# A two-layer convolution and expert-retrieval encoder on one core: the first stage reordered, the adaLN rows in column tiles, the pooling on TensorE

## The reference, cut to what matters

```python
mod = silu(c) @ w_ada[l] + b_ada[l]                  # 1024 -> 6*1024: sh1, sc1, g1, sh2, sc2, g2
h = rmsnorm(x, norm_mix_g[l]) * (1 + sc1) + sh1
# layer 0
p = h @ w_in                                         # 1024 -> 512 + 512 + 512
a = a_lin * sigmoid(a_gate)
a_conv = depthwise_causal_conv(concat(prev_a, a), dw_a) + db_a        # 31 taps
a_out = silu(layernorm(a_conv, ln_g, ln_b))
pooled = multiscale_pool(concat(prev_b, b_in)) - b_in                 # means over 2, 4, 8, 16 tokens, by group
b_out = einsum('btgc,gcd->btgd', pooled, w_pool) * pool_scale         # (near the start the mean is over fewer)
y = concat(a_out, b_out) @ w_out
x = x + g1 * y
h = rmsnorm(x, norm_ffn_g[l]) * (1 + sc2) + sh2
x = x + g2 * peer(h, wq, k1, k2, u, v)               # queries, top-16 keys, gelu(u.h), weighted sum of v
```

## Time and profile before

| what | before |
|---|---|
| median of 3 runs | 4036.21 us (4035.36 to 4036.81) |
| the profiled execution | 4037.75 us |
| its span | 4036.0 us |
| mean granted TensorE clock | 0.973 |
| PE busy | 3816.7 us (95%) |
| PEld busy | 2994.3 us (74%) |
| DVE busy | 2563.5 us (64%) |
| ACT busy | 1024.1 us (25%) |
| POOL busy | 120.8 us (3%) |

### The profile page before, as it was taken

How to read it: one execution, slowest core, us unless ns; L and a number is a source line. 1 busy time by engine, 2 the same in 40 slices (tenths; PEclk the granted TensorE clock), 3 DMA queues, 4 the chain that set the end, 5 groups by cost and what they waited for, 6 DMA issues and landing times.

```text
span 4036.0 us, 72731 instructions
## 1 busy us (share of the span) xinstructions
PE 3816.7 (95%) x31704; PEld 2994.3 (74%) x31704; DVE 2563.5 (64%) x3885; ACT 1024.1 (25%) x950; POOL 120.8 (3%) x61
## 2 busy tenths in 40 slices
PE   8819889999999999999997989999999999999998
PEld 2302468888888888888883548888888888888886
DVE  1370277556665588888874438556566758888886
ACT  1300133332333311111113123333333321111111
POOL 0190000000000000000000000000000000000000
PEclk9859989999999999999998989999999999999999
DMA  7305222454654764545431311436456484545450
GB/s 277 126 23 196 87 84 90 177 187 154 212 188 157 273 240 190 212 184 198 181 134 63 116 64 64 147 137 206 165 204 198 168 322 183 200 182 215 183 192 33
DMA packets 196223, 667.08 MB, mean 165 GB/s; under 512 B 11952, under 2 KB 151360, under 8 KB 152512
## 3 DMA queue, kind: packets, MB, share of 16 engines
q1 hardware_dynamic: 190608, 663.67, 44.6%
q10 hardware_dynamic: 5392, 0.56, 0.1%
q0 software_dynamic: 32, 0.01, 0.0%
HBM read 514.72 MB, written 149.49 MB: 165 GB/s over the span
## 4 chain that ended last, share of the span: by engine, by line
PE 91%; DVE 3%; POOL 3%; DMA 2%; ACT 1%; issue 0%; SPq 0%; DVEq 0%; ACTq 0%; POOLq 0%
PE PS L691 35%; PE PS L647 33%; PE PS L568 5%; PE PS L622 5%; PE PS L591 4%; PE PS L551 3%; PE PS L677 3%; POOL arena L1016 2%; DVE ring L1096 1%; PE PS L578 1%; DMA arena<-gates_dram 1%; PE PS L635 1%; PE PS L597 1%; DMA arena<-act_dram 1%; DVE stat L1071 0%; ACT H L782 0%
## 5 line engine op out<-in xcount | busy, mean ns | idle before, releaser
L647 PE MATMUL PS<-X,ring 128*128 128x272 f16 x12288 | 1436.9, 279 | 0.0
L691 PE MATMUL PS<-arena,ring 128*128 128x272 f16 x12288 | 1423.7, 279 | 2.9 <-DVE ring L1096 2.9
L691 PEld LDWEIGHTS PS<-arena,ring 128*128 128x128 f16 x12288 | 1202.2, 98 | 224.4 <-issue 3.5
L647 PEld LDWEIGHTS PS<-X,ring 128*128 128x128 f16 x12288 | 1198.8, 98 | 218.7 <-issue 0.4
L1096 DVE SCALAR_TENSOR_TENSOR ring<-ring 128x4096 f16<-128x4096 f32 x145 | 641.3, 4424 | 634.8 <-ACT ring L791 626.3
L791 ACT ACTIVATE ring<-ring 128x4096 f16<-128x4096 f32 x145 | 523.9, 3615 | 1119.6 <-PE PS L691 1119.6
L1365 DVE TENSOR_TENSOR ACC<-PS,ACC 128x544 f32<-128x544 f32 x512 | 362.9, 719 | 237.1 <-PE PS L691 237.1
L921 ACT ACTIVATE H<-PS 128x544 f32<-128x544 f32 x256 | 159.9, 625 | 974.3 <-PE PS L647 974.3
L1355 DVE TENSOR_TENSOR arena<-arena 128x544 f32<-128x544 f32 x256 | 292.1, 1141 | 46.0 <-DMA arena<-act_dram 46.0
L622 PE MATMUL PS<-X,ring 128*128 128x272 f16 x1536 | 188.1, 284 | 38.2 <-DVE X L1103 38.2
L622 PEld LDWEIGHTS PS<-X,ring 128*128 128x128 f16 x1536 | 150.2, 99 | 73.2 <-issue 43.9
(11 more groups left out here) (136 smaller groups left out, 1821.8 us busy)
## 6 DMA issues: line engine op xcount, KB each, us to landing
ring<-U SPq DMA_DIRECT2D x64, 2048.0 KB, 10.5
ring<-V SPq DMA_DIRECT2D x64, 2048.0 KB, 7.9
act_dram<-H SPq DMA_DIRECT2D x64, 1088.0 KB, 5.0
gates_dram<-ACC SPq DMA_DIRECT2D x68, 1024.0 KB, 5.7
arena<-gates_dram SPq DMA_DIRECT2D x32, 2176.0 KB, 9.5
arena<-act_dram SPq DMA_DIRECT2D x64, 1088.0 KB, 5.1
ring<-whole_w SPq DMA_DIRECT2D x28, 2048.0 KB, 7.8
ring<-split_w SPq DMA_DIRECT2D x17, 2048.0 KB, 7.8
```

What stands on the lines that cost most here:

```text
L647: mm = pe.matmul(ps_halves(u)[:, half, :], parts[lane][:, pu, k * 512 + j * P:k * 512 + (j + 1) * P], H16[:, ph, k, half * HALF:(half + 1) ...
L691: mm = pe.matmul(ps_halves(u)[:, half, :], parts[lane][:, pv, j * D + c * P:j * D + (c + 1) * P], WT[:, grp, pw, j, half * HALF:(half + 1) ...
```

## The change

The first stage gets another order, and three of its parts another form.

- TensorE runs four adaLN slots (`EARLY`: `sh1` and `sc1` of layer 0), then five chunks of the input projection (`LEAD`), then seven more with one slot ahead of each (`BETWEEN`), then the other thirteen slots. `mod` of both layers is finished by `rest_of_mod` on VectorE behind the LayerNorm.
- The rows of a slot go to four column tiles: the conditioning vectors are padded with zeros to 32 columns, and k goes to the PSUM partitions 32 (k mod 4) and on. The turning product adds the four tiles up, with a 128 x 2 pick matrix in place of the identity.
- The convolution runs in two halves of two channel chunks, the first as soon as chunks 0, 1, 4 and 5 are read.
- GpSimd no longer pools. TensorE adds up shifted products of EB with `w_pool`/window (and `w_pool`/window - `w_pool` for the unshifted one); the first 16 tokens, where the mean is over fewer, go through a small pooled copy that VectorE makes (`corners`).
- The output projection does the half over the pooling channels (k 4 to 7) of its first four chunks ahead of and between the LayerNorm's sums; `Z` from VectorE completes them.
- adaLN slots past the fourth land in four places of their own (`ada_at`: two in the arena, H, and ring slot 1). The keys' tile holds the small tables until the keys are loaded, which waits for the last turn. The two split lanes change places.

```diff
+EARLY = 4
+LEAD = (0, 1, 2, 4, 5)
+BETWEEN = (3, 6, 7, 8, 9, 10, 11)
+POOL_AFTER = {13: 0, 14: 1, 15: 2, 17: 3}
...
# SyncE
+            def load_ada(s):
+
+                i = s % 4
+                if s >= EARLY + 4:
+                    sp.wait_ge(mm_done, ROW_AT[s - 4] + 1)
+                sp.dma_start(ada_at[i], whole_w[s]).then_inc(ada_in[i], 16)
...
+                    for f in range(EARLY):
+                        load_whole(f, f, None)
                     for lane in range(2):
-                        load_raw(lane, split_w[3 + lane], None)
+                        sp.wait_ge(mm_done, ROW_AT[lane] + 1)
+                        load_raw(lane, split_w[lane], None)
+                    load_ada(EARLY)
+                    load_ada(EARLY + 1)
+                    load_raw(0, split_w[2], 1)
+                    sp.wait_ge(hm_split, KD)
+                    load_ada(EARLY + 2)
+                    sp.wait_ge(split[1], 1)
+                    for s in range(EARLY + 3, 20):
+                        load_ada(s)
+                    for i in range(2):
+                        load_whole(2 + i, 2 * ADA_SLOTS + i, CHUNK_AT[11] + 1)
+                    load_raw(0, split_w[3], 2)
+                    for s in range(20, 2 * ADA_SLOTS):
+                        load_ada(s)
+                    sp.wait_ge(mm_done, ROW_AT[2 * ADA_SLOTS - 1] + 1)
+                    load_raw(1, split_w[4], None)
+                    sp.wait_ge(mm_done, ROW_TURNED[2 * ADA_SLOTS - 1] + 1)
...
# TensorE
+            def ada_rows(s):
...
+                u = begin("act")
+                for k in range(KD):
+                    at = k % 4 * 32
+                    mm = pe.matmul(PS[at:at + 32, u % PAIRS, 0:512], cact[:, k, :], wt[:, k * 512:(k + 1) * 512],
+                                   start=(k < 4), stop=(k >= 4))
+                mm.then_inc(mm_done, 1)
+
+            def ada_turn(s):
+
+                u = begin("act")
+                pe.wait_ge(act_read, ROW_AT[s])
+                for m in range(4):
+                    mm = pe.matmul(ps(u)[:, 2 * m:2 * m + 2], mod_rows[:, s % 2, m * P:(m + 1) * P], pick_row,
+                                   start=True, stop=True)
+                mm.then_inc(mm_done, 1)
+
+            def pool_branch(g):
+
+                u = begin("act")
+                wnd = WINDOWS[g]
+                pe.wait_ge(act_read, CHUNK_AT[8 + g])
+                pe.matmul(ps(u)[:, 0:CORNER], wpool[:, g, :], PL[:, g, :], start=True, stop=True)
+                for a, b, s in ((CORNER, NP_, 0), (NP_, T, 1)):
+                    o = EB_PAD * (1 + s)
+                    for i in range(wnd):
+                        mm = pe.matmul(ps(u)[:, a:b], WP[:, g, int(i == 0), :], EB[:, g, a + o - i:b + o - i],
+                                       start=(i == 0), stop=(i == wnd - 1))
+                mm.then_inc(mm_done, 1)
...
+                    for s in range(EARLY):
+                        ada_rows(s)
+                        if s:
+                            ada_turn(s - 1)
+                    ada_turn(EARLY - 1)
+                    split_ready(0)
+                    for c in LEAD:
+                        if c == 4:
+                            split_ready(1)
+                        project_chunk(0, c // 4 % 2, c, (lambda k: pe.wait_ge(hm_split, k + 1)) if c == 0 else None)
+                    for n, c in enumerate(BETWEEN):
+                        ada_rows(EARLY + n)
+                        if n:
+                            ada_turn(EARLY + n - 1)
+                        if c == 8:
+                            split_ready(0)
+                        project_chunk(0, c // 4 % 2, c)
                     pe.wait_ge(pool_in, 16)
...
+                    for s in range(EARLY + len(BETWEEN), 2 * ADA_SLOTS):
+                        ada_rows(s)
+                        ada_turn(s - 1)
+                        if s in POOL_AFTER:
+                            pe.wait_ge(wp_ready, 1)
+                            pe.wait_ge(corner_ready, 1)
+                            pool_branch(POOL_AFTER[s])
+                    ada_turn(2 * ADA_SLOTS - 1)
+
+                    u_sum, u_sq, u0, u1 = (begin("dve") for _ in range(4))
+                    pe.wait_ge(act_read, POOL_AT[KA - 1])
+                    wt = slot_ready(2)
+                    project(u0, wt, 0, range(KA, KD), True, False)
+                    project(u1, wt, 1, range(KA, KD), True, False)
+                    column_sums(u_sum, CONV, KA, conv_ready, 1, EA_PAD)
+                    column_sums(u_sq, SQ, KA, sq_ready, KD + 1)
+                    u2 = begin("dve")
+                    project(u2, wt, 2, range(KA, KD), True, False)
+                    u3 = begin("dve")
+                    project(u3, wt, 3, range(KA, KD), True, False)
+                    for m, u in enumerate((u0, u1, u2, u3)):
+                        project(u, wt, m, range(KA), False, True, lambda k: pe.wait_ge(z_ready, k + 1)).then_inc(mm_done, 1)
+                    wt = slot_ready(3)
+                    for m in range(4):
+                        project(begin("dve"), wt, m, range(KD), True, True).then_inc(mm_done, 1)
...
# ScalarE
+                    take_turn(EARLY - 1)
+                    high(0, U_SCALE)
+                    act.wait_ge(mod_ready, 1)
+                    modulate(l, 0)
+                    high_part(H, HM[l], h_ready, 1, hm_high)
+                    high(1, U_SCALE)
...
+                        if c == 3:
+                            high(0, U_SCALE)
+                            act.wait_ge(pool_in, 16)
+                            for g, wnd in enumerate(WINDOWS):
+                                for first in range(2):
+                                    ins = act.activation(WP[:, g, first, :], wpool[:, g, :], ACT.Copy, scale=1.0 / wnd - first)
+                            ins.then_inc(wp_ready, 1)
...
# VectorE
+                    dve.wait_ge(act_read, ROW_TURNED[EARLY - 1])
+                    link(mod_part(0, 0, 2))
+                    scale_part(0, 0).then_inc(mod_ready, 1)
+                    low(0, U_SCALE)
+                    low_part(H, HM[l], hm_high, hm_split)
+                    low(1, U_SCALE)
...
+                    for first in (0, 2):
+                        for c in (first, first + 1):
+                            glu(c)
+                        dve.wait_ge(glu_ready, first + 2)
+                        for i in range(WA):
+                            for c in (first, first + 1):
...
+                            if first == 0 and i == 8:
+                                low(0, U_SCALE)
+                            if first == 0 and i == 24:
+                                corners()
```

More of the change, by code:

```diff
@@ L533, in from_turn_before @@
                     last[(w.use.n + i) % PAIRS] = (reader, count.at(i - PAIRS + 1))
[L535 to L570, removed]
@@ L572, in column_sums, with slot_ready, project @@
-            def column_sums(src, chunks, semaphore, value, gap=0):
-                u = begin("dve")
+            def slot_ready(i):
+                arrived[i] += 1
+                pe.wait_ge(slot_in[i], arrived[i] * 16)
+                return ring[:, i, :]
+            def project(u, wt, m, ks, start, stop, ready=None):
+                for k in ks:
+                    if ready is not None:
+                        ready(k)
+                    for a, b, _ in SEG:
+                        mm = pe.matmul(ps(u)[:, a:b], wt[:, k * 512 + m * P:k * 512 + (m + 1) * P], Z[:, k, a:b],
+                                       start=(start and k == ks[0]), stop=(stop and k == ks[-1]))
+                return mm
@@ new lines, in project_chunk @@
+            def project_chunk(l, lane, c, ready=None):
+                u = begin("act" if c < 16 else "dve")
+                m = c % 4
+                for k in range(KD):
+                    if ready is not None:
+                        ready(k)
+                    for n, (pw, ph) in enumerate(PASSES):
+                        for a, b, _ in SEG:
+                            mm = pe.matmul(ps(u)[:, a:b], parts[lane][:, pw, k * 512 + m * P:k * 512 + (m + 1) * P],
+                                           HM[l][:, ph, k, a:b], start=(k == n == 0), stop=(k == KD - 1 and n == 2))
+                mm.then_inc(mm_done, 1)
@@ L575, in column_sums, with split_ready @@
+            def split_ready(lane):
+                lanes[lane].n += 1
+                pe.wait_ge(split[lane], lanes[lane].at())
+            def column_sums(u, src, chunks, semaphore, value, gap=0):
                 for k in range(chunks):
@@ L601, in ada @@
[L601 to L605, removed]
-                from_turn_before("act")
+            def ada_rows(s):
+                if s < EARLY:
+                    wt = slot_ready(s)
+                else:
+                    wt = ada_at[s % 4]
+                    pe.wait_ge(ada_in[s % 4], 16 * (s // 4))
+                u = begin("act")
+                for k in range(KD):
```

(5 more changed lines are left out.)

396 lines of the change are left out of this document (196 added, 200 removed).

## The result

The changed kernel takes 3844.22 us (median of 4 runs, 3837.36 to 3846.09) against 4036.51 (4 runs); ratio 0.9521, 95% interval 0.9504 to 0.9537. The profiled execution took 3843.43 us with a span of 3841.6, 194.4 less than before. All but 0.7 us of it lies in the first stage: the output projection ends at 302.5 us instead of 496.2, 193.7 earlier.

What follows compares the result with a forecast made beforehand. TensorE was taken as the bound, except while GpSimd pooled beside the convolution. Stage end 222.7 + 9.0 + 4.5 + 18.0 + 54 = 308.2 against 496.2, 188 us less: 3849.8 profiled, 3848 forecast; range 3830 to 3900.

Steps and rivals of the forecast that it cites:

- the start of the projection: Head of the stage: after four slots, split and modulation, the input projection starts at 49.0 us instead of 134.67.
- five chunks: Input projection: the first five chunks, without slots between them, take 31.2 us, to 80.2.
- the slots' end with its last reading: Thirteen slots with 34 us of pooling products on TensorE: through at 222.7 us, last turn and reading included.
- the tail: From the slots' end to the output projection's end: 9.0 + 4.5 + 18.0 + 54 us, ending at 308.2.
- The price of a slot: Row products of one adaLN slot on TensorE: 2.2 us instead of 6.96, all four column tiles running at once.
- The terms for the stagger and the last pass's end: Within a slot's 2.2 us: 3 x 0.09 for staggered tile starts and 0.2 for the last pass's end, beside 1.74.
- the rule of strict program order: Rival at the slots' rows: program order holds across tiles, 3.9 us a slot, 3888 us in all; chance 0.13.
- Convolution and cover: VectorE stands from about 122 till 144 for chunk 11, ends at 202; TensorE's sums at 232 leave 30 us.
- TensorE, not the queue, sets this end: End of the thirteen slots: slot 23 lands by 213, TensorE is through at 222.7, so transfers do not set it.
- A sign that was to mean wrong: TensorE idle before a slot's rows, with a transfer as the releaser, would show the forecast wrong.
- The rival of the queue: From slot 8 on, transfers come singly at 7.8 us instead of 5.0 and set the slots: 3859 us; chance 0.09.
- The slower rival: TensorE's 241 us from first chunk to stage end run at 1.2 GHz: 4089 us, slower by 53; chance 0.03.

Runs made afterwards that it cites:

- the experiment in one piece: Changed kernel with all four gates first and the convolution as 31 taps over four chunks instead of two halves: 3839.36 us (0.9508).
- The swap: Kernel before with only the second 12 adaLN slots moved ahead of the pooled products, no tiles, pooling still on GpSimd: 3944.16 us (0.9770).
- Tiles alone: Kernel before with the slots' rows in four column tiles and nothing else of the change: 3952.31 us (0.9787).
- the reorder alone: Changed kernel with all eight products of a slot's rows in column tile 0, everything else as changed: 3959.26 us (0.9807).
- the profile with 1.00: Later profile of the unaltered changed kernel, granted clock 1.00 instead of 0.86 around the LayerNorm: span 3835.2 us, stage end 296.5.
- the late loads: Changed kernel with two output-projection slots and a split weight queued behind slot 23: 3840.91 us; without 26 of 30 pooling taps 3826.05; with VectorE pooling, sums first 3826.31.

## Why the prediction was right, point by point

**Forecast and sum.** 3848 forecast, 3844 measured; stage end 308.2 against 302.5. The terms: the start of the projection 49.0 against 49.13; five chunks 31.2 against 31.71; the twelfth chunk done at 143.3 against 140.4; the slots' end with its last reading 222.7 against 214.3; the tail 85.5 against 88.2. So 308.2 came within 6 us with two errors of opposite sign, 8.4 too long up to the end of the slots and 2.7 too short behind it. The rest of the kernel moved by 0.7 us (194.4 of span less 193.7).

**The price of a slot.** 2.2 and two switches of 0.1 were taken, 1.85 to 1.90 came with the switches in it; 4 x 0.435 = 1.74 would be the floor. The terms for the stagger and the last pass's end were too much: from the start of a slot's rows to the start of the turn behind them the chain has 1.85, which leaves 0.11 for both and the switches. Over 20 slots that is 11 us, more than the 8.4 at the slots' end; the other way went the five chunks (0.5), the wait for slot 23 (1.2) and its rows at the lower clock (1.7). That four tiles run side by side was read rightly from the order of lines 661 and 663; with passes of 512 columns the overlap is 3.7-fold. By the rule of strict program order of the Trainium skill (TensorE: Matmul & The Clock Gate, Part 3) a slot would have taken an estimated 3.9 us; the trace disagrees, with 1.9.

**Convolution and cover.** The wait for chunk 11, the end (202 against 197.8) and the time to spare (30 against 31.44) came as forecast, and the experiment in one piece shows that the early start of the first half had no use.

**What failed.** "TensorE, not the queue, sets this end": the queue stood right behind it. I had slot 23 landing at 213 and TensorE ready at 222.7 and called the difference a verdict; with the cheaper slots TensorE arrived at about the time of the landing, and 28 us of products less changed the time by less than the runs lie apart. The transfer of slot 23 had been taken at its 7.8 us alone; it took 10.57 from the release by slot 19's rows. A sign that was to mean wrong, TensorE idle before rows with a transfer as the releaser, did come, for 1.2 us. The forecast did not suffer, since both bounds lay within 10 us of each other. The rival of the queue had been priced at 3859 with single transfers at 7.8 us; queued, they kept 5.0.

**What was only half seen.** I put the 94 us between projection and second block down to the pooling on GpSimd. The swap shows that one block's place in the program order stood between the kernel before and nearly half of the gain (93 of 195). Tiles alone gave 85, the reorder alone 78 (117 short of both together); 163 in sum against 195 together. The tiles are thus worth 117 on top of the reorder and 85 without it, where slot transfers stand uncovered on the chain. The stage's tail took 2.7 us more than forecast: the granted clock dips around the LayerNorm in this profile (0.86 in 205:255), and in the profile with 1.00 it took 84 us.

**The slower rival** (the clock at half for three quarters of the stage) did not come: 0.95 to 1.00 in the windows from 50 to 200. The clock did fall behind them, in the four places named above, which cost 6 us in one profile and nothing in the other.

## What to carry to other kernels

When an engine idles beside a long job elsewhere, look first at what stands at the head of its program and whether the work behind needs it: that one swap was worth nearly half of this large change. When two bounds lie within some per cent of each other, here TensorE's work and a queue of weight slots, taking one away shows little; remove both, and judge neither by an experiment on it alone. A transfer on the chain of waits is as long as the transfer; what it costs is in the wait of the engine it releases.

## What the runs showed of the hardware

- f32 products whose outputs lie in four different 32-partition tiles run side by side: 16 passes of 512 columns in 1.9 us, against 6.98 in one tile, each pass still shown with 0.592 us of its own. These 1.9 us are at a granted clock of 1.00; at 0.52 they were 3.57.
- Slots of 2048 KB land every 4.9 to 5.0 us when several are queued (419 GB/s, 429 in a 10 us window), at the head of the kernel and beside VectorE's convolution alike.
- The issue of one small transfer on ScalarE's queue took 2.78 us before, 3.44 in the changed kernel, 4.45 without the shifted products, and 10.83, 13.18 and 13.16 in the three kernels with the late loads, without the shifted products, with them, and with the pooling on VectorE. So the length goes with the late loads, which put weight transfers in flight at that time, and not with the shifted products. What holds the issue was not tested.
- Between two runs of one kernel the clock near short waits of TensorE came out at 0.86 or 1.00 for the same 50 us, which moved the end of the stage by 6 us.
- One addition of 128 x 573 on GpSimd took 85.15 us while VectorE convolved (85.15 and 85.14 in two other kernels) and 1.11 us behind it. What holds it beside VectorE was not tested.
